# Where 128 table transposes are placed among the stages of a fused two-block layer kernel

## The reference

```
h = rms_norm(x); aq,ak,av,hq,hf,hi,hg,ga,gh = split(h @ w_in)     # first stage, 22 panels of 128 columns
y_attn = sliding_window_attention(aq, ak, av, sinks)              # window attention
o = hgrn2_recurrence(silu(hq), hf, hi, lower_bound)               # recurrence, chunks of 32 tokens
y_hgrn = rms_norm(o) * silu(hg)
merged = sigmoid(ga)*(y_attn @ w_attn_proj) + sigmoid(gh)*(y_hgrn @ w_hgrn_proj)
x = x + merged @ w_out                                            # merge
x = x + peer_layer(rms_norm(x), w_peer_q, peer_keys, peer_u, peer_v)
```

## Time and profile before

| | us |
|---|---|
| median of 3 runs | 2236.32 (2236.14 to 2239.86) |
| profiled execution, its own time | 2242.32 |
| its span, first to last instruction | 2240.5 |
| VectorE busy | 1503.6 (67%) |
| TensorE busy | 1937.5 (86%) |
| 128 turns, busy | 155.8 |
| idle of VectorE just before turns | 101.1 |

### The profile page before, as it was taken

How to read it: one execution, slowest core, us unless ns; L and a number is a source line. 1 busy time by engine, 2 the same in 40 slices (tenths; PEclk the granted TensorE clock), 3 DMA queues, 4 the chain that set the end, 5 groups by cost and what they waited for, 6 DMA issues and landing times. The chain is left out here.

```text
span 2240.5 us, 24715 instructions
## 1 busy us (share of the span) xinstructions
PE 1937.5 (86%) x8290; PEld 1320.4 (59%) x8290; DVE 1503.6 (67%) x3103; ACT 517.9 (23%) x1206; POOL 921.2 (41%) x694
## 2 busy tenths in 40 slices
PE   6987789979778989988888989988896669998987
PEld 4864468758556856655555555555552247754565
DVE  5468745469989877776666666666667888335544
ACT  3345122222227800010000000000000032335641
POOL 2432034323120265565555545545556613323442
PEclk9998589989889999999999999999998879999998
DMA  7988979579463899999999999999999933201002
GB/s 255 391 323 274 305 283 386 211 287 325 156 259 151 320 389 406 406 406 406 407 407 406 406 406 405 406 407 408 406 405 403 358 117 99 67 19 38 1 1 75
DMA packets 187277, 648.83 MB, mean 290 GB/s; under 512 B 19600, under 2 KB 35984, under 8 KB 185872
## 3 DMA queue, kind: packets, MB, share of 16 engines
q1 hardware_dynamic: 101760, 336.32, 39.6%
q0 software_dynamic: 73728, 268.47, 30.3%
q10 hardware_dynamic: 11664, 42.47, 5.5%
HBM read 561.20 MB, written 85.98 MB: 289 GB/s over the span
## 5 line engine op out<-in xcount | busy, mean ns | idle before, releaser
L1818 PE MATMUL ps<-arena 128*128 128x512 f32 x1024 | 498.7, 633 | 126.5 <-DVE arena L1648 111.2
L1659 DVE CUSTOM_DVE_ANT_0 arena<-arena 128x1024 bf16<-128x1024 f32 x256 | 313.5, 1225 | 306.1 <-DMA arena<-u_rows,u_row 184.1
L1807 PE MATMUL ps<-rows_n,arena 128*128 128x256 f32 x2048 | 472.5, 380 | 1.0 <-DMA arena<-in_u 1.0
L1807 PEld LDWEIGHTS ps<-rows_n,arena 128*128 128x128 f32 x2048 | 384.1, 190 | 98.3 <-issue 52.9
L1818 PEld LDWEIGHTS ps<-arena 128*128 128x128 f32 x1024 | 197.1, 200 | 374.7 <-issue 217.8
L1443 POOL DMA_INDIRECT arena<-u_rows,u_row x256 | 302.3, 1181 | 198.1 <-DVE u_row L1525 84.8
L1443 POOL DMA_INDIRECT arena<-in_v,expert x192 | 199.4, 1038 | 306.4 <-DVE arena L1680 274.6
L1680 DVE SCALAR_TENSOR_TENSOR arena<-arena,wt 128x1024 f32<-128x1024 f32 x192 | 245.8, 1280 | 0.4
L1782 ACT ACTIVATE ge<-dots 128x2 f32<-128x2 f32 x128 | 26.0, 203 | 865.0 <-DVE dots L1659 865.0
L193 DVE STREAM_TRANSPOSE tdst<-tsrc 128x1024 f32<-128x1024 f32 x128 | 155.8, 1231 | 101.1 <-DMA tsrc<-in_u 49.4
L246 POOL TENSOR_TENSOR in_wlo<-in_raw,in_whi 128x1024 fp32r<-128x1024 f32 x45 | 113.6, 2526 | 241.7 <-ACT in_whi L234 161.5
(11 more groups left out here) (455 smaller groups left out, 2832.6 us busy)
## 6 DMA issues: line engine op xcount, KB each, us to landing
tsrc<-in_u SPq DMA_DIRECT2D x128, 512.0 KB, 7.9
u_rows<-tdst SPq DMA_DIRECT2D x128, 512.0 KB, 6.5
arena<-in_u SPq DMA_DIRECT2D x128, 512.0 KB, 8.9
arena<-in_v SPq DMA_DIRECT2D x128, 512.0 KB, 7.5
in_raw<-in_panels ACTq DMA_DIRECT2D x37, 512.0 KB, 4.4
gates<-arena SPq DMA_DIRECT2D x8, 2048.0 KB, 9.3
arena<-gates SPq DMA_DIRECT2D x15, 1024.0 KB, 19.1
mg_raw<-in_panels ACTq DMA_DIRECT2D x28, 512.0 KB, 6.7
```

The source lines that it names most:

```text
L1659: nc.vector.tensor_tensor_reduce(out=junk[:, n % 2], in0=u_slot[n % NU], in1=hrows[:, n // NPICK], scale=1.0, scalar=0.0, op0=ALU.mult, op ...
L1807: mm = nc.tensor.matmul(ps[:, j % 2, 0:TD], ud[:, j % RJ, k], rows_n2[:, 0, k], start=k == 0, stop=k == KD - 1)
L1818: mm = nc.tensor.matmul(ps[:, 4 + 2 * t + c], park[:, j % NPK, t * P:(t + 1) * P], vd[:, j % RJ, c * T:(c + 1) * T], start=j == 0, stop=j ...
```

## The change

```diff
-TURNS = 34, 14, 17, 40, 0, 23
+TURNS = 36, 14, 8, 47, 0, 23
@@
-        places = [4 * m for m in range(KD - 2) for x in range(4)] + [4 * KD - 4] * 2 + [4 * KD + 2 * m + 1 for m in range(KD - 4) for x in range(2)]
+        places = [4 * m for m in range(KD) for x in range(4)] + [4 * KD + 2 * m + 1 for m in range(KD - 4) for x in range(3)]
```

## The result

The changed kernel takes 2243.20 us, median of 20 runs (2235.06 to 2252.22), beside 2237.56 for the kernel before on the same chips (20 runs, 2232.17 to 2243.82). The ratio is 1.0029, 95% interval 1.0020 to 1.0039: some 6.5 us slower (the medians differ by 5.6). The prediction was 2236.2, no change, with a range up to 2242.5. The gains in its sum came about as forecast, its two costs were too small, and one more, taken at 0, was there.

What follows compares the result with a forecast made beforehand. Bound by place: full DMA engines in the first stage and behind output panels 2 and 3, VectorE's turns on the recurrence's path. -4.64 - 0.5 + 2.0 + 0 + 0 + 3.0 = -0.1, so 2236.2 us; 8 in 10: 2230 to 2242.5.

Steps and rivals of the forecast that it cites:

- The gains in its sum: Recurrence with fewer turns on the path, -4.64 us, and less traffic ahead of the merge's first panels, -0.5.
- its two costs: Extra turns in the first stage, +2.0 us, and behind the output panels, +3.0 us.
- one more, taken at 0: Merge's last group, five turns instead of two: lateness of 0.7 us vanishes in a cast; 0, ends 0 and 2.
- Recurrence, -4.64 and -0.5: Recurrence, 17 turns to 8: four on the path at 1.16 us each; less traffic before the merge, -0.5.
- First stage, +2.0: First stage, 34 turns to 36: copy slips 4.9 us, less 2.5 for a transfer hole; 2.0 taken.
- The merge's last group, 0: Group 7, five turns: 0.7 us late, hidden by a cast that ends with GpSimd's subtraction; 0.
- Output panels, +3.0: Behind output panels, 10 turns to 13: five more transfers, 5.1 us later, less 2.08 spare on VectorE.
- The rival "paid in full": First stage, last group, outputs: turns where DMA is full cost 4.9, 0.7 and 4.2; +4.7, 2241.0 us; chance 0.18.
- The third rival: Recurrence gains nothing, TensorE's half-clock products set its pace; +4.4, 2240.7 us; chance 0.05.
- more than 5 us at the first stage or the outputs: Sign of being wrong: first stage or outputs move by more than 5 us.
- the last group's cast would still end with GpSimd's: Sign, merge's group 7: five turns end by 424 and the cast still ends with GpSimd's subtraction.

Runs made afterwards that it cites:

- e4: Kernel before with 13 turns behind the output panels instead of 10, three fewer in the merge's groups; 1.0032 of before.
- e2: Kernel after with 34 turns in the first stage instead of 36 and 49 in the merge instead of 47; 1.0013 of before.
- e10: Kernel after with the ten loads during the output panels' turns cut to 64 of 1024 columns, part of the table wrong; 0.9994 of before.
- e1: Kernel after with 10 turns behind the output panels as before, and 37 in the merge's groups; 1.0005 of before.
- e3: Kernel before with the same 17 recurrence turns moved to other chunks, none behind c = 4t; 1.0006 of before.
- e6: Kernel after with 34 turns in the first stage, 39 in the merge's groups and 10 behind the outputs, keeping 8 in the recurrence; 0.9979 of before.
- e7: Kernel after with the 13 output turns placed 4, 4, 4, 1 instead of 3, 3, 3, 4; 1.0021 of before.

## Why the prediction was wrong

- *Recurrence, -4.64 and -0.5: right, a little high.* 70.8 against 75.3 on average is -4.5, before to after -4.8, of the -5.14 forecast. The turns behind c = 4t were on the path, by 0.93 each in the third tile where I took 1.16; the others were in the wait for ScalarE. ScalarE's wait for the merge's first panel is gone in after.
- *First stage, +2.0: mis-sized, the first step that failed.* It measured +5.1 (six traces against six), a little over the upper end of 4.9; before to after alone it is +3.5. In that pair the sum can be done again. TensorE's gap grew by 3.8: 4.9 for the slip to the next turn, less 1.8, because that turn came so much earlier, counted from the stage's first product (72.9 us, before 74.7), plus 0.7, because L794 took 2.99 us where it had taken 2.25. I had set 2.9 against the 4.9, for 2.5 us of unused transfer time behind the running sum and for deep queues. Part of the hole only moved: after has these three stretches,

```profile
100.00:103.00 3.00, 3.00 (x15) 2.46 (x14) 1.83 (x2) 0.36 (x1) 1.76 (x1) 1.00 1.02 416
103.00:106.00 3.00, 3.00 (x15) 2.49 (x14) 1.25 (x1) 0.70 (x1) 2.22 (x1) 1.00 1.03 382
106.00:109.00 3.00, 3.00 (x15) 2.49 (x14) 2.58 (x3) 0.93 (x1) 0.18 (x1) 1.00 1.01 249
```

  and 249 GB/s are again 1.2 us lost in three, where the earlier trace rows had 277 and 212. Over these nine us 1.5 are lost, before 2.9 (with 359 GB/s in the third stretch). The rest of the +5.1 is that before is the slowest of the six traces with 34 turns, and the only one with a gap ahead of L750: I read one execution's gap as the kernel's. I also priced one of the two turns at nothing. 2 turns x 1.05 MB at 417 GB/s would be 5.0 us, close to the measured step, but the step from 32 turns (114.5, one trace) to 34 is 1.8, and one trace with 36 has 118.4. So what one turn costs there isn't settled.
- *The merge's last group, 0: wrong by some 1.7.* Traces with five turns in it have groups of 139.6 us, the others 137.9; no run changes this alone. The fifth waited 6.48 us for a store: that of the second turn, which ended at 409.2, had landed only by 421.1, 11.9 us where I took 8.2, with the DMA engines busy up to it. The shortened cast hid some 2 us, as the prediction said it would, but the lateness was 4.3 us, not 0.7: L1142 starts at 422.85, before at 422.96, while GpSimd's subtraction starts 4.4 us earlier than before. By the Trainium skill ("SBUF — State Buffer", section "Who interferes with whom") the loser waits for the whole of the winner's instruction; after shows the other side of it, a cast of 0.43 us once GpSimd is through.
- *Output panels, +3.0: mis-sized, the second step that failed, and the largest.* The last of these turns starts 7.6 to 9.2 us later, counted from the first of them, where I took 5.1 (5 transfers at full rate, less an early start). I let the queues begin sooner and gave 1.16 back; without that the 6.3 stands beside 7.6 in e4. The rate is not full throughout: 24 transfers of 0.524 MB in 37.6 us are 334 GB/s in after, 19 in 28.4 are 351 before. Outputs +5.6 on average, 7.2 in after. In after one square took 2.92 us for 0.69, beside GpSimd's subtraction of 2.40 us from 462.48; that explains at most 2.2 of the 7.2, and e2 and e4, where that square took 0.69, have 52.9 and 52.1 us. The 0.5 to 0.9 us of the slow mean I hadn't thought of.
- *The sum.* -4.5 + 5.1 + 1.7 + 5.6 = 7.9 by the traces' averages, beside 6.5 (4.5 to 8.7) measured. The rival "paid in full", at 0.18, had the outcome and the place. Its price of 4.7 lies at the low end of the interval: its 4.9 for the first stage is what was measured, its 4.2 for the outputs and 0.7 for the last group were too low. That the full DMA engines set the price is shown for the outputs, by e10, and not for the first stage. (The third rival's 4.9 should read 5.0, from 2.0 and 3.0; it changes nothing.)
- *The signs.* I had named more than 5 us at the first stage or the outputs as what would refute me; the outputs' 7.2 did. That the last group's cast would still end with GpSimd's didn't come true either.

Behind the merge the spans differ by several us from one execution to the next (before 1752.5 from the first `pq` product on, after 1748.2, e4 1756.5), so what the change does there isn't settled by single traces.

## What to carry to other kernels

Side work has the price of the resource that is full where it is put. Behind the output panels that was its bytes, at the rate that the stretch really reaches. Holes in the view of the DMA rate shouldn't be counted as free time: of the 2.9 us that the stretch from 100 to 109 us left unused before, after still has 1.5, at another place. Where a latency-bound chain leaves an engine idle, the place within the chain decides, until the pieces loaded ahead run out. And a wait that a forecast starts from should be looked for in more than one execution.

## What the runs showed of the hardware

The granted clock in the attention changes from run to run though its instructions don't: over 161 to 213 us it was 0.84 in before and after, 0.90 in e1, 0.71 in e3, and e3's attention took 55.0 us where e1's took 52.3. In e3 the low clock reached into the recurrence: its first products of L1021 take 1.91 us, in before 1.06, TensorE in order of time in e3:

```profile
216.18 1.91 PE L1021 MATMUL ps<-hq,kinv 128*128 128x128 f32 x8
```

Over all thirteen traces the attention takes 51.6 to 56.5 us. The clock isn't the whole of it: with 0.76 e6 has the 56.5, with 0.75 e7 has 53.5. So a single trace can be off by a few us there. In no run did fewer turns lift the clock of the recurrence's later tiles: over 229 to 262 us it is 0.50 or 0.51 in all thirteen.
